# Half-section convolutions and an activation by hyperbolic tangent in a gated delta-rule layer

## The reference, cut to what matters

```
proj = h @ w_in            # q, k, v, z of the delta rule, q, k, v of a window attention, two gates
q = causal_conv_silu(q);  k = causal_conv_silu(k);  v = causal_conv_silu(v)
#   y[t] = x[t-3]*w0 + x[t-2]*w1 + x[t-1]*w2 + x[t]*w3 ;  silu(y) = y * sigmoid(y)
q = q * rsqrt(sum(q*q) + 1e-6);  k = k * rsqrt(sum(k*k) + 1e-6)      # per head of 128
o = gated_delta_rule(q, k, v, g, beta)
y_b = window attention of 16 heads, computed over the same tokens, with a sink in the softmax
```

## Time and profile before

| what | value |
|---|---|
| median of three runs | 1751.0 us (1748.91 to 1752.21) |
| the profiled execution: own time, span | 1750.58 us, 1748.8 us |
| PE busy | 1707.3 us, 98% of the span |
| DVE, ACT, POOL busy | 1170.1, 922.3, 212.1 us |
| mean granted clock of TensorE | 0.996 |
| memory read | 267.23 MB, 153 GB/s over the span |

### The profile page before, as it was taken

One profiled execution on the slowest core, in us unless ns is written; L12 is line 12 of the kernel. 1 busy time (PEld: TensorE's weight loads), 2 busy tenths in 40 slices (PEclk: granted clock), 3 DMA queues, 4 the chain that ended last, 5 costly groups with the idle time before them and its releaser, 6 DMA issues.

```text
span 1748.8 us, 28216 instructions
## 1 busy us (share of the span) xinstructions
PE 1707.3 (98%) x10753; PEld 1403.6 (80%) x10753; DVE 1170.1 (67%) x2216; ACT 922.3 (53%) x1696; POOL 212.1 (12%) x334
## 2 busy tenths in 40 slices
PE   9999999999999999999999999999999999999998
PEld 7878878888788788877777778888887787878887
DVE  5655667766566676677867776666677867776655
ACT  5355375453554754557545455555567545455553
POOL 1201200022030000311202000000301202000000
PEclk9999999999999999999999999999999999999999
DMA  8543544555444445633333455554633322455552
GB/s 294 166 164 125 169 132 157 188 178 193 140 135 160 137 155 178 219 121 97 121 98 98 146 172 187 185 186 161 216 121 98 120 98 98 146 171 184 185 185 92
DMA packets 137133, 270.10 MB, mean 154 GB/s; under 512 B 5548, under 2 KB 8744, under 8 KB 137000
## 3 DMA queue, kind: packets, MB, share of 16 engines
q1 hardware_dynamic: 134928, 265.44, 45.2%
q10 hardware_dynamic: 2072, 2.86, 0.5%
HBM read 267.23 MB, written 1.05 MB: 153 GB/s over the span
## 4 chain that ended last, share of the span: by engine, by line
PE 83%; DVE 6%; ACT 4%; issue 3%; POOL 3%; DMA 0%; ACTq 0%; DVEq 0%; POOLq 0%
PE bank L421 20%; PE bank L423 20%; PE bank L422 20%; PE bank L402 5%; PE bank L445 3%; PE bank L404 3%; DVE buf L2018 2%; DVE lo L384 1%; POOL scratch L965 1%; PE bank L1677 1%; PE bank L1654 1%; PE bank L607 1%; PE bank L1620 1%; ACT hi L374 1%; DVE buf L2016 1%
## 5 line engine op out<-in xcount | busy, mean ns | idle before, releaser
L421 PE MATMUL bank<-hi,xhl 128*128 128x512 f32 (+1 forms) x1792 | 725.4, 405 | 5.8 <-issue 2.9
L423 PE MATMUL bank<-hi,xhl 128*128 128x512 f32 (+1 forms) x1792 | 698.9, 390 | 0.0
L422 PE MATMUL bank<-lo,xhl 128*128 128x512 f32 (+1 forms) x1792 | 696.5, 389 | 0.0
L374 ACT ACTIVATE hi<-raw 128x1024 fp32r<-128x1024 f32 (+1 forms) x504 | 519.9, 1051 | 235.7 <-PE bank L423 217.4
L384 DVE TENSOR_TENSOR lo<-raw,hi 128x1024 fp32r<-128x1024 f32 (+1 forms) x504 | 606.0, 1220 | 55.1 <-PE bank L423 39.5
L421 PEld LDWEIGHTS bank<-hi,xhl 128*128 128x128 f32 x1792 | 337.5, 188 | 78.8 <-issue 15.3
L423 PEld LDWEIGHTS bank<-hi,xhl 128*128 128x128 f32 x1792 | 336.7, 188 | 73.0
L422 PEld LDWEIGHTS bank<-lo,xhl 128*128 128x128 f32 x1792 | 338.1, 189 | 60.0
L402 PE MATMUL bank<-xhl,hi 128*128 128x512 f32 x384 | 136.0, 398 | 0.0
L404 PE MATMUL bank<-xhl,lo 128*128 128x256 f32 x384 | 107.8, 281 | 0.0
L402 PEld LDWEIGHTS bank<-xhl,hi 128*128 128x128 f32 x384 | 72.1, 188 | 17.8
(11 more groups left out here) (316 smaller groups left out, 1855.2 us busy)
## 6 DMA issues: line engine op xcount, KB each, us to landing
raw<-in_w_in SPq DMA_DIRECT2D x135, 1024.0 KB, 5.1
raw<-in_w_ff SPq DMA_DIRECT2D x64, 1024.0 KB, 5.3
raw<-in_w_proj_a SPq DMA_DIRECT2D x8, 1024.0 KB, 5.1
raw<-in_w_proj_b SPq DMA_DIRECT2D x8, 1024.0 KB, 5.0
raw<-in_w_out SPq DMA_DIRECT2D x8, 1024.0 KB, 5.4
raw<-in_w_up_sw SPq DMA_DIRECT2D x8, 1024.0 KB, 5.0
raw<-in_w_up_dn SPq DMA_DIRECT2D x8, 1024.0 KB, 5.1
raw<-in_w_o SPq DMA_DIRECT2D x8, 1024.0 KB, 5.1
```

What stands on the lines that cost most here:

```text
L374: act.activation(self.hi[g % HI_RING][:, 0:w], src, ACT.Copy).then_inc(self.hi_ready, 1)
L421: pe.matmul(out, xh[:, row, t], self.hi[slot % HI_RING][:, w], start=first, stop=False)
L422: pe.matmul(out, xh[:, row, t], self.lo[slot % LO_RING][:, w], start=False, stop=False)
L423: mm = pe.matmul(out, xl[:, row, t], self.hi[slot % HI_RING][:, w], start=False, stop=last)
```

## The change

The four turns of a section now stand so that the first two need only the first job of the section: `turn dk 0` and `dk 1` inside dk1, `dk 2` and `dk 3` inside dq0, `dq 0` and `dq 1` inside dq1, and so on. Turn f goes to bank f. The activation is written as y * (1 + tanh(y/2)), which is twice silu: ACT makes the tangent of two head blocks (128x512) into a scratch tile, POOL adds 1 to it and multiplies (two instructions). The factor of two is taken back in the 0.5 of the value path and in the epsilon of the norms.

```diff
-                         [("turn", "sk", 0)], turns("sq")[0], turns("sq")[1] + turns("sq")[2], turns("sq")[3] + work[0]])
-    conv = lambda n: [[("turn", n, (0, 2, 4, 6).index(i))] if i in (0, 2, 4, 6) else [] for i in range(8)]
-    p.run(sec("dq", 0), [b + a for a, b in zip(conv("dk"), work[1:9])][:7] + [work[8] + [("silu", "dk")]])
-    norms = [[], [("square", "dk")], [], [("squares", "dk")], [], [("squares_turn", "dk")], [], [("scales",)]]
-    p.run(sec("dv", 2 * D), [c + a + b for a, b, c in zip(work[9:17], conv("dq"), norms)])
+                         turn("dk", 0), turn("sk", 0) + turn("dk", 1), turn("sq", 0) + turn("sq", 1) + [("silu", "dk", 0)],
+                         turn("sq", 2) + turn("sq", 3) + work[0] + [("silu", "dk", 1)]])
+    conv = lambda old, new: [turn(old, 2), [], turn(old, 3) + [("silu", old, 2)], [], [("silu", old, 3)], turn(new, 0), [],
+                             turn(new, 1) + [("silu", new, 0)]]
+    sums = [[], [], [], [], [], [], [("square", "dk")], []]
+    p.run(sec("dq", 0), [c + a + b for a, b, c in zip(work[1:9], conv("dk", "dq"), sums)])
+    norms = [[("squares", "dk")], [("silu", "dq", 1)], [("squares_turn", "dk")], [], [("scales",)], [], [("square", "dq")], []]
+    p.run(sec("dv", 2 * D), [c + a + b for a, b, c in zip(work[9:17], conv("dq", "dv"), norms)])
...
-    put(2, ("silu", "dq"))
-    put(3, ("square", "dq"))
-    put(7, ("squares", "dq"))
-    put(9, ("squares_turn", "dq"))
+    put(3, ("squares", "dq"))
+    put(7, ("squares_turn", "dq"))
...
-    put(21, ("silu", "dv"))
-    for at, name, n in ((1, "dv", 0), (10, "dv", 1), (12, "dv", 2), (17, "dv", 3), (21, "kd", 0), (27, "ys", 0),
+    for f, at in ((1, 2), (2, 5), (3, 9)):
+        put(at, ("silu", "dv", f))
+    for at, name, n in ((1, "dv", 2), (5, "dv", 3), (21, "kd", 0), (27, "ys", 0),
...
+TURN_BANK = {("dv", 0): 0, ("dv", 1): 1, ("dv", 2): 2, ("dv", 3): 3,
...
-                    a = qT_(conv_out[arg][0])
-                    act.wait_ge(*at("convolved", (arg, 3)))
-                    act.activation(a, a, ACT.Silu).then_inc(*up("silu", arg))
+                    f = what[2]
+                    act.wait_ge(*at("convolved", (arg, f)))
...
+                    act.activation(silu_tanh[f % 2], qT_(conv_out[arg][0])[:, 2 * f:2 * f + 2, :], ACT.Tanh, scale=0.5)\
+                       .then_inc(*up("silu_tanh", (arg, f)))
...
+                if kind == "silu":
+                    f = what[2]
+                    a = qT_(conv_out[arg][0])[:, 2 * f:2 * f + 2, :]
+                    pool.wait_ge(*at("silu_tanh", (arg, f)))
+                    pool.tensor_scalar(silu_tanh[f % 2], silu_tanh[f % 2], 1.0, None, ALU.add).then_inc(*up("silu", (arg, f, "factor")))
+                    pool.wait_ge(*at("silu", (arg, f, "factor")))
+                    pool.tensor_tensor(a, a, silu_tanh[f % 2], ALU.mult).then_inc(*up("silu", (arg, f)))
```

More of the change, by code:

```diff
@@ L1102, in plan_two @@
     work = [w[:1] + w[:0:-1] if len(w) == 3 else w for w in attention("s", HEADS)]
+    turn = lambda name, f: [("turn", name, f)]
     p.run(sec("dk", D), [[("rope", "sk", 0), ("rope", "sk", 1), ("rope", "sq", 0)], [("rope", "sq", 1)], [], [],
-                         [("turn", "sk", 0)], turns("sq")[0], turns("sq")[1] + turns("sq")[2], turns("sq")[3] + work[0]])
-    conv = lambda n: [[("turn", n, (0, 2, 4, 6).index(i))] if i in (0, 2, 4, 6) else [] for i in range(8)]
-    p.run(sec("dq", 0), [b + a for a, b in zip(conv("dk"), work[1:9])][:7] + [work[8] + [("silu", "dk")]])
-    norms = [[], [("square", "dk")], [], [("squares", "dk")], [], [("squares_turn", "dk")], [], [("scales",)]]
-    p.run(sec("dv", 2 * D), [c + a + b for a, b, c in zip(work[9:17], conv("dq"), norms)])
+                         turn("dk", 0), turn("sk", 0) + turn("dk", 1), turn("sq", 0) + turn("sq", 1) + [("silu", "dk", 0)],
[6 more added lines that the diff above has]
+    p.run(sec("dv", 2 * D), [c + a + b for a, b, c in zip(work[9:17], conv("dq", "dv"), norms)])
     slots = delta_slots(work[17])
@@ L1186 @@
               "delta_u": OUT, "delta_s": TURN, "delta_r": OUT, "delta_v": TURN, "delta_o": OUT}
-TURN_BANK = {("dv", 0): 2, ("dv", 1): 0, ("dv", 2): 1, ("dv", 3): 2,
+TURN_BANK = {("dv", 0): 0, ("dv", 1): 1, ("dv", 2): 2, ("dv", 3): 3,
+             ("sk", 0): OUT, ("sq", 0): TURN, ("sq", 1): OUT, ("sq", 2): TURN, ("sq", 3): OUT,
              ("v", 0): 0, ("v", 1): 1, ("v", 2): OUT, ("v", 3): OUT, ("kd", 0): 2, ("kd", 1): 0,
              ("ys", 0): 0, ("ys", 1): 1, ("ys", 2): 0, ("ys", 3): 1,
[2 rows of a table removed]
[2 rows of a table added]
 SQUARES_BANK = {"dk": TURN, "dq": OUT}
@@ L1398, in block_two @@
     mid_row = qd[:, 0, 0:S]
+    silu_tanh = [scr[:, 3072 + 512 * i:3584 + 512 * i].rearrange("p (n t) -> p n t", n=2) for i in range(2)]
+    silu_order = [(name, f) for name in ("dk", "dq", "dv") for f in range(4)]
+    silu_before = dict(zip(silu_order[2:], silu_order))
     def ended(plan, name):
@@ L1496, in _ @@
                     wait = {"sq": ("rotated", "sq"), "sk": ("rotated", "sk"),
-                            "dq": ("conv_in", "dq1"), "dk": ("conv_in", "dk1"), "dv": ("conv_in", "dv1"),
+                            "dq": ("conv_in", f"dq{f // 2}"), "dk": ("conv_in", f"dk{f // 2}"), "dv": ("conv_in", f"dv{f // 2}"),
                             "ys": ("ys", HEADS - 1), "yd": ("yd_gated", f), "mix": ("mix", f // 2),
-                            "v": ("silu", "dv"), "kd": ("silu", "dk")}.get(arg) or ("evac", f"up{arg[1:]}")
+                            "v": ("silu", ("dv", f)), "kd": ("silu", ("dk", 3))}.get(arg) or ("evac", f"up{arg[1:]}")
                     pe.wait_ge(*at(*wait))
@@ L1615, in _ @@
                     if arg == 0:
-                        pe.wait_ge(*at("silu", "dk" if kind == "gram" else "dq"))
+                        pe.wait_ge(*at("silu", ("dk" if kind == "gram" else "dq", 3)))
                     for i, (j, c) in enumerate(HC):
@@ L1805, in _ @@
                 if kind == "silu":
-                    a = qT_(conv_out[arg][0])
-                    act.wait_ge(*at("convolved", (arg, 3)))
-                    act.activation(a, a, ACT.Silu).then_inc(*up("silu", arg))
+                    f = what[2]
+                    act.wait_ge(*at("convolved", (arg, f)))
+                    if (arg, f) in silu_before:
+                        act.wait_ge(*at("silu", silu_before[arg, f]))
+                    act.activation(silu_tanh[f % 2], qT_(conv_out[arg][0])[:, 2 * f:2 * f + 2, :], ACT.Tanh, scale=0.5)\
+                       .then_inc(*up("silu_tanh", (arg, f)))
                 if kind == "squares":
@@ L1812, in _ @@
                 if kind == "square":
-                    act.wait_ge(*at("silu", arg))
+                    act.wait_ge(*at("silu", (arg, 3)))
                     if arg == "dq":
@@ L2026, in _ @@
                             h = 2 * f + j
-                            ins_ = dve.tensor_tensor(vb[:, :, h * DV:h * DV + DV],
-                                                     B[core.turn_bank[s.stage, arg, f]][:, j * S:j * S + S].rearrange("p (t d) -> p t d", d=DV),
-                                                     bcast(t.beta[:, :, h], 2, DV), ALU.mult)
+                            ins_ = dve.scalar_tensor_tensor(vb[:, :, h * DV:h * DV + DV],
+                                                            B[core.turn_bank[s.stage, arg, f]][:, j * S:j * S + S].rearrange("p (t d) -> p t d", d=DV),
+                                                            0.5, bcast(t.beta[:, :, h], 2, DV), ALU.mult, ALU.mult)
                         ins_.then_inc(*up("turn_copied", (arg, f)))
@@ L2315, in _ @@
                     if arg == "dq":
-                        rsqrt(pool, s, core, t.ssq2, t.rq, DV, 1e-6 * DV, "rq_mean", "rq", 0)
+                        rsqrt(pool, s, core, t.ssq2, t.rq, DV, 4e-6 * DV, "rq_mean", "rq", 0)
                     else:
-                        rsqrt(pool, s, core, t.ssq2, t.rk, 1.0, 1e-6, "rk_mean", "rk", 0)
+                        rsqrt(pool, s, core, t.ssq2, t.rk, 1.0, 4e-6, "rk_mean", "rk", 0)
                 if kind == "gram":
```

## The result

| what | before | changed |
|---|---|---|
| median | 1750.74 us (1748.91 to 1752.21, 4 runs) | 1776.47 us (1773.56 to 1777.01, 4 runs) |
| profiled execution: own time, span | 1750.58, 1748.8 us | 1776.59, 1774.8 us |
| mean granted clock of TensorE | 0.996 | 0.988 |

The ratio is 1.0144, with its interval 1.0127 to 1.0162: slower by 25.7 us, where 16 were forecast.

The account below looks back on a forecast made before the run. PE, busy 98%, was taken as the bound: new waits of 26.7 us less 15.6 old gave +11.1, the clock +4.65, on 1750.6 making 1766.3, stated as 1767 us. The range was 1754 to 1777.

Parts of the forecast that it names:

- The doors: Ahead of dv0 and gb0, PE waits for the convolution into bank 1: 3.7 us, twice a layer, 14.8 us in all.
- What goes: PE's old waits behind convolutions, the rotation and ACT in the changed stretch all vanish: 15.6 us for both layers.
- The waits of heads: PE waits where delayed convolutions make head chains late, beyond 0.4 us of room; four cases, (A) to (D).
- (A): POOL's activation dk 1 between heads 0 and 1 delays DVE: PE waits 1.6 us in slot dq0.2 (0.8 to 3.5).
- (B): POOL's power of the norms in dv0.2 delays convolution dq 3: PE waits 1.9 us at dv1, next head 0.65.
- (C): Convolution dv 0 in slot dv1.1 makes the last head's turn wait: 0.7 us a layer (0 to 2.5).
- (D): In gb, dv 3 is convolved behind DVE's gram work, so gb1 waits: 1.1 us a layer (0 to 3.7).
- The clock: PE falls to 1.2 GHz behind each of four 3.7 us waits, 1.55 us each, less one old fall: +4.65 us.
- Rival 1: POOL is slow, each activation 4.3 us under the lock; 5.5 us more per layer, 1778 us; chance 0.13.
- Rival 2: The clock falls no more often than before; 1762 us; chance 0.17.
- Rival 3: The 3.7 us waits let ACT and DVE catch up, so (A) to (D) are nothing; 1747 us; chance 0.07.
- Rival 4: The doors' 14.8 us come, (A) to (D) only a third, falls after two doors; 1756 us; chance 0.13.

Follow-up runs that it names:

- open doors: Changed kernel with the turns back in slots 0, 2, 4 and 6, a whole piece ahead of the job needing bank 1: 1756.16 us, ratio 1.0022.
- first four versions: Open doors, filled doors, later activation, and before with tanh in place of silu (no table loads); before measured again beside them: 1751.67 us.
- later activation: Changed kernel with POOL's activation of dk 1 moved behind head 1's instructions, to the end of slot dq0.0: 1770.32 us, ratio 1.01.
- product alone: Changed kernel without POOL's addition of 1, multiplying with the bare tangent (value not silu): 1766.9 us, ratio 1.0097.
- filled doors: Changed kernel with 14 discarded 512-column matmuls on PE ahead of dv0 and gb0, the wait for bank 1 kept: 1768.70 us, ratio 1.0093.

## Why the prediction was right, and where its size was off

**The doors: right.** 3.73 us four times, against 3.7 forecast from the earlier trace rows. That open doors remove them shows the cause.

**What goes: right.** All 15.6 us of the old waits went. Without the loads alone 5.9 went; the rest went with the moved turns, which no run took one by one.

**The waits of heads.** (A) was 2.42 and 2.44, forecast 1.6: POOL's one-input operation was taken as 0.7 us, chosen between the ends 0.20 and 1.29, and takes 1.50, above the upper end without a lock. The 0.8 us more than assumed are the 0.8 us more of wait, and without that operation the wait is 0.68. (B) was 1.71 and 1.72, forecast 1.9, with 0.52 in the first layer's next output (0.65 forecast, none in the second layer). (C) was 0.96 and 0.49 (0.7). (D) was 1.45 and 1.42 (1.1). One wait was not seen: 0.51 ahead of L1567, the turn of the sums, in both layers. It is POOL's too: it is gone where the addition is left out. With some 0.1 ahead of head 0's turn in each layer the sums are 15.1 and 14.2 us a layer, 29.3 together, where 26.7 were forecast. Net of the 15.6 that is +13.7 against +11.1. Two readings behind (B) and (D) were loose, without weight for the result: a piece is 2.7 us by the earlier trace rows, not 2.8, and PE's arrival at gb1 after 17.9 us stands in no row. In the changed kernel it comes 20.8 us after gb's begin, some 2.8 of them the low clock's.

**The clock: right in kind, and the term that was mis-sized.** The forecast had 4.65 us. Of the 25.7 measured, 13.7 are idle time, so 12.0 are left, and PE's busy time grew by 11.7. Two steps of the forecast's sum were too small. It priced each door at one fall as after 1398.20, 1.55 us. Measured, the low level at a door lasted 6.8 us instead of the 3.4 there, and cost 2.1 to 2.8 us a door by the rows. And it left the falls after shorter waits out of the sum and kept them for the upper end (+10.8): three came, two at (A) and one at dv1, 3 x 1.55 = 4.65. Both old falls, 3.1, went; of them the forecast had one, and the other stood behind a wait of 1.99 us that is still there, so the change did not take it away. That makes 9.8 + 4.65 - 3.1 = 11.4 us. But before had a third low stretch, near its start, where the changed kernel had none:

```profile
9.00:13.00 4.00, 4.00 (x21) 3.92 (x20) 2.98 (x5) 3.36 (x7) 0.00 (x0) 0.57 1.05 393
...
949.27:952.70 3.43, 3.43 (x103) 2.75 (x104) 1.58 (x2) 1.61 (x3) 0.00 (x0) 1.00 0.19 27
```

With its 1.55 us off, 9.8 of the 12.0 are accounted for, and some 2 stay unexplained. Runs of one kernel differ by as much: those of before beside the first four versions had spans from 1746.4 us at a clock of 0.998 to 1751.9 at 0.995. The second row is behind the fourth of before's waits near 1.9 us, at 949.27; the prediction counted three, of which two brought a fall, and it is two of four. In the changed kernel it is three of six waits from 1.7 to 2.4 us, but all four of 3.7, and all eight of that length in the versions with the later activation and with the product alone.

"TensorE: Matmul & The Clock Gate" (Part 1) of the Trainium skill says that idleness takes the clock down and work brings it back. The filled doors agree, 1.00 behind them instead of 0.60; what a wait of a given length costs was to be had only here.

**The rivals.** Rival 1, slow POOL, gave 1778, nearer to the time than the forecast, but by another way: POOL's activation took 2.85 us as a rule and not 4.3, and (C) was no 2.5. (A) at 2.4 lies between the forecast's 1.6 and the rival's 3.5, by the plain length of the addition. Rival 2, no falls, is out by the rows. Rival 3 is out: (A) to (D) all came. Rival 4 is out: all four doors had their full 3.7, and (A) to (D) came whole. So the mechanism was that of the forecast, with (A) and the clock too small. That the time still fell into the range is partly luck: the range reached to 1777 for rival 1's sake, and what filled it was the clock.

## What to carry to other kernels

A step that produces what the next job's first instruction needs must stand at least one full piece ahead of it: four turns standing directly ahead of their job cost 14.9 us of wait and by the rows 9.8 of low clock here (20.3 in all by the open doors), about three times the 6.8 us that the twelve table loads had cost. Price a wait of the bounding engine as its length and the slow stretch behind it, here 3.7 us of wait and another 2 to 3; waits of 1.7 to 2.4 us brought 1.55 us more in five of ten cases in the two kernels. Work given to an engine that is 12% busy on average still has a place in its list: ask what small instruction stands behind it, and who waits for that.

## What the runs showed of the hardware

POOL's addition of a constant to 128x512, one input, takes 1.50 us and its product of two such tiles 1.28. The Trainium skill ("GPSIMD Engine Reference", section 4.1) calls two-input operations there about twice as slow as VectorE's and one-input ones roughly line-rate, so one would expect the one-input form to be the faster of the two; here it is the slower.

The lock that the prediction spoke of was seen to hold up DVE as well as POOL. Two rows of DVE's timeline in the changed kernel:

```profile
751.19 2.33 DVE L384 TENSOR_TENSOR lo<-raw,hi 128x1024 fp32r<-128x1024 f32 x1
...
796.15 1.22 DVE L384 TENSOR_TENSOR lo<-raw,hi 128x1024 fp32r<-128x1024 f32 x1
```

And what POOL did beside them:

```profile
751.17 1.27 POOL L2330 TENSOR_TENSOR buf<-buf,scratch 128x512 f32<-128x512 f32 x1
...
796.23 2.27 POOL L2330 TENSOR_TENSOR buf<-buf,scratch 128x512 f32<-128x512 f32 x1
```

Where POOL began first, at 751.17, DVE's low part took 2.33 us instead of 1.22; where DVE began first, at 796.15, POOL's product took 2.27 instead of 1.27. For POOL it is the exception: four of the 24 products and two of the 24 additions took over 2 us, against medians of 1282 and 1496 ns. DVE was held more often: nine of its low parts in the two layers' stretches took 1.51 to 2.33 us; in the kernel before the longest took 1.52.
